# A router fed from the raw residual: logits scaled by rstd after the matmul, half of a multiply moved to GpSimd

## The reference, cut to what matters

```python
x = x + mod[:, None, 2] * y                       # y: the mixer's output
h = modulate(rmsnorm(x, norm_ffn[i]), mod[:, 3], mod[:, 4])
x = x + mod[:, None, 5] * moe(h, w_router, b_router, w_exp_gate[i], w_exp_up[i], w_exp_down[i])

def rmsnorm(x, g):  return x * rsqrt(mean(x * x, -1) + eps) * g
def modulate(h, shift, scale):  return h * (1.0 + scale) + shift

def moe(h, ...):
    scores = sigmoid(x @ w_router)                # x is h; T = 384 tokens, 16 experts
    sel = scores + b_router                       # best group of four, then its top two
    ...
    hid = silu(x @ wg[e]) * (x @ wu[e]);  y = sum_e combine[t, e] * (hid @ wd[e])
```

## Time and profile before

| | us |
|---|---|
| three runs | 1322.2, 1330.95, 1330.68; median 1330.68 |
| the profiled execution | 1324.39 |
| its span in the profile | 1322.7 |
| TensorE busy | 1200.5 (91%) |
| VectorE, ScalarE, GpSimd busy | 383.4, 316.7, 122.6 |
| mean granted TensorE clock | 0.962 of full speed |

### The profile page before, as it was taken

How to read it: one execution, slowest core, us unless ns; L and a number is a source line. 1 busy time by engine, 2 the same in 40 slices (tenths; PEclk the granted TensorE clock), 3 DMA queues, 4 the chain that set the end, 5 groups by cost and what they waited for, 6 DMA issues and landing times.

```text
span 1322.7 us, 24788 instructions
## 1 busy us (share of the span) xinstructions
PE 1200.5 (91%) x10404; PEld 697.5 (53%) x10404; DVE 383.4 (29%) x1218; ACT 316.7 (24%) x716; POOL 122.6 (9%) x188
## 2 busy tenths in 40 slices
PE   4788998789998899899978999999999997789996
PEld 2446544447885554654447643445465444565544
DVE  1345111340004522621132023341451115561113
ACT  1240111231124522211133211230411114401113
POOL 2000100210000000111020000000002111001101
PEclk9898999889999999899989999999999998989998
DMA  9999999794326873898979223891689987658993
GB/s 349 412 421 421 409 413 421 282 350 151 119 96 247 298 314 140 321 409 347 412 271 351 69 96 106 357 363 64 251 344 357 419 359 277 273 214 355 397 390 136
DMA packets 89708, 389.57 MB, mean 295 GB/s; under 512 B 10456, under 2 KB 38604, under 8 KB 53240
## 3 DMA queue, kind: packets, MB, share of 16 engines
q1 hardware_dynamic: 71568, 336.61, 65.2%
q0 software_dynamic: 17456, 51.07, 10.5%
q10 hardware_dynamic: 568, 0.23, 0.1%
HBM read 370.96 MB, written 27.96 MB: 302 GB/s over the span
## 4 chain that ended last, share of the span: by engine, by line
PE 76%; DMA 10%; DVE 5%; SPq 3%; issue 3%; ACT 2%; POOL 1%; POOLq 0%; DVEq 0%; ACTq 0%
PE bank L491 70%; DMA sb_ring<-in_w_ada 3%; PE bank L966 3%; SPq L449 2%; DMA slot_out<-sb_arena,sb_homes 2%; DMA sb_arena<-slot_out,sb_slots 2%; DMA sb_ring<-in_w_exp_up 2%; POOL sb_arena L2132 1%; DVE sb_xT L1994 1%; PE bank L984 1%; DMA slot_out<-sb_arena 1%; DMA sb_arena<-token_rows,sb_rows 1%; PE bank L894 0%; DVE sb_arena L1954 0%; PE bank L1017 0%
## 5 line engine op out<-in xcount | busy, mean ns | idle before, releaser
L491 PE MATMUL bank<-sb_ring,sb_arena 128*32 128x256 f32 (+1 forms) x6112 | 449.9, 429 | 17.3 <-DMA sb_ring<-in_w_exp_down 8.0
L491 PEld LDWEIGHTS bank<-sb_ring,sb_arena 128*32 128x32 f32 x6112 | 212.5, 111 | 197.8 <-issue 108.0
L491 PE MATMUL bank<-sb_arena 128*128 128x128 f32 (+11 forms) x776 | 140.7, 361 | 10.9 <-DVE sb_arena L1840 7.0
L491 PE MATMUL bank<-sb_ring,sb_hT 128*128 128x256 f32 x624 | 140.8, 387 | 6.2 <-ACT sb_hT L1225 6.2
L491 PEld LDWEIGHTS bank<-sb_ring,sb_hT 128*128 128x128 f32 x624 | 120.6, 194 | 26.9 <-issue 9.1
L491 PEld LDWEIGHTS bank<-sb_arena 128*128 128x128 f32 (+2 forms) x776 | 102.7, 194 | 45.6 <-issue 13.0
L491 PE MATMUL bank<-sb_ring,sb_cond 128*2 128x512 f32 x768 | 94.9, 616 | 8.8 <-DMA sb_ring<-in_w_ada 8.5
L491 PE MATMUL bank<-sb_arena,sb_ring 128*128 128x384 f32 (+2 forms) x288 | 95.5, 507 | 3.0 <-DVE sb_arena L1710 2.1
L1941 DVE TENSOR_TENSOR sb_arena<-sb_arena,bank 128x256 f32<-128x256 f32 x40 | 16.8, 421 | 248.9 <-PE bank L491 248.9
L491 PE MATMUL bank<-sb_hT,sb_ring 128*128 128x384 f32 x256 | 85.8, 498 | 2.6 <-ACT sb_hT L1225 2.6
L491 PEld LDWEIGHTS bank<-sb_arena,sb_ring 128*128 128x128 f32 (+1 forms) x288 | 49.9, 181 | 44.9 <-issue 19.0
(11 more groups left out here) (318 smaller groups left out, 1013.8 us busy)
## 6 DMA issues: line engine op xcount, KB each, us to landing
sb_ring<-in_w_ada SPq DMA_DIRECT2D x96, 1024.0 KB, 8.7
sb_ring<-in_w_exp_gate SPq DMA_DIRECT2D x60, 1024.0 KB, 10.4
sb_ring<-in_w_exp_up SPq DMA_DIRECT2D x60, 1024.0 KB, 12.7
sb_ring<-in_w_exp_down SPq DMA_DIRECT2D x60, 1024.0 KB, 15.1
sb_ring<-in_w_mlstm_in SPq DMA_DIRECT2D x12, 1024.0 KB, 12.1
token_rows<-sb_arena POOLq DMA_DIRECT2D x12, 512.0 KB, 7.6
slot_out<-sb_arena POOLq DMA_DIRECT2D x9, 512.0 KB, 8.8
sb_scratch<-in_w_exp_gate SPq DMA_DIRECT2D x4, 1024.0 KB, 9.0
```

The costliest lines, as they stand in the source:

```text
L491: return pe.matmul(out, lhsT, rhs, start=first, stop=last)
```

## The change

The router no longer waits for `hT`. A scaled router matrix `w_ra` (`w_router` times the gain, one for context and one for latents, 32 columns) is made on VectorE ahead of the residual (`router_weights`); the shift's part of the logits is made by 16 small matmuls (`shift_logits`) and kept in a row (`shift_copy`). TensorE multiplies the raw residual by `w_ra`, between the sums of squares (`raw_logits`). When `rstd` is there, VectorE multiplies the logits by it (`norm_routed`) and TensorE folds them, with the shift's part added by three matmuls. VectorE then multiplies only chunks 0 to 3 of `xT` by `rstd`, over all tokens at once, and GpSimd chunks 4 to 7 (`hp_scaled`); ScalarE applies gain and shift together (`modulate`), chunk 0 ahead of the router's exponential, the rest behind it. The turns go in the order 0, 2, 4 (chunks 0 to 3), the counts of the picks (five matmuls in place of nine), then 1, 3, 5. The modulation rows 4, 5 and 6 now stand together behind the turns. In the diff the first pieces are TensorE's, `modulate` and the `experts` below it ScalarE's, `router_weights` and the `norm_routed` below it VectorE's, and the last `experts` GpSimd's; `TURNS` is [0, 2, 4, 1, 3, 5]. Some semaphores are merged.

```diff
+            def raw_logits(L, n, a, b):
+                pe.wait_ge(wra_ready, L + 1)
+                for k in range(a, b):
+                    pe.wait_ge(x_ready, 8 * n + k + 1)
+                    q = k % 4
+                    ins = mm(ps[5][32 * q:32 * q + 32, 0:TOK], w_ra[:, k, :, :].rearrange("p c e -> p (c e)"), xT[:, k, :],
+                             k < 4, k >= 4)
+                    if k >= 4:
+                        ins.then_inc(lg_full, 1)
+
+            def shift_logits(L, bank):
+                pe.wait_ge(mod_added, 3 * L + 2)
+                for c in range(2):
+                    for k in range(KC):
+                        ins = mm(bank[0:1, c * NE:(c + 1) * NE], mod[:, L, 24 + k, c:c + 1], w_rt[:, k, :], k == 0, k == KC - 1)
+                ins.then_inc(sr_full, 1)
+
+            def norm_routed(L, n):
+                if L == 0:
+                    norm(n)
+                    ada(2, 6, 7)
+                    ada_columns(2)
+                    shift_logits(0, ps[5])
+                    raw_logits(L, n, 0, KC)
+                else:
+                    for a, b in ((0, 2), (2, 4), (4, 6), (6, 7), (7, 8)):
+                        raw_logits(L, n, a, b)
+                        norm_squares(n, a, b)
+                    norm_mean(n)
+                pe.wait_ge(sr_ready, L + 1)
+                for t in range(NT):
+                    c = min(t, 1)
+                    mm(ps[4][:, t * NE:(t + 1) * NE], ones[0:1, :], shift_row[:, c * NE:(c + 1) * NE], t == 0, False)
+                pe.wait_ge(lg_ready, L + 1 + (L > 0))
+                for t in range(NT):
+                    c = min(t, 1)
+                    ins = mm(ps[4][:, t * NE:(t + 1) * NE], lg[:, t * P:(t + 1) * P], fold[:, c * NE:(c + 1) * NE], False, t == NT - 1)
+                ins.then_inc(rt_full, 1)
...
             def pool_mixer(r):
+                if r:
+                    shift_logits(3, ps[7])
...
                 pe.wait_ge(hsT_ready, 8)
                 pe.wait_ge(n_copied, 1)
+                shift_logits(1, ps[5])
...
             def mla(r):
+                shift_logits(2, ps[7])
...
             def experts(L, n):
-                side(ps[6], w_rt, n)
-                for c in range(2 * NT):
-                    if c == 2:
-                        unfold(ps[6], L + 1 + (L > 0), rt_full)
+                def count_picks():
+                    pe.wait_ge(mask_ready, L + 1)
+                    pick = rt[:, 5, :]
+                    sums = ps[6][:, 64:64 + (NT + 1) * NE]
+                    mm(sums[:, NE:], ones[:, :], pick, True, False)
+                    mm(sums[:, 0:NE], tri[:, 0:P], pick[:, 0:NE], False, False)
+                    mm(sums[:, NE:NT * NE], tri[:, 0:P], pick[:, NE:], False, False)
+                    mm(sums[:, 2 * NE:], ones[:, :], pick[:, 0:2 * NE], False, False)
+                    mm(sums[:, NT * NE:], ones[:, :], pick[:, 0:NE], False, True).then_inc(pos_full, 1)
+
+                for c in TURNS:
+                    if c == 1:
+                        count_picks()
+                    pe.wait_ge(h_ready, 16 * n + (8 if c % 2 == 0 else 16))
+                    if c == 4:
+                        pe.wait_ge(rt_e, L + 1)
                     for k in range(4):
                         ins = pe.transpose(ps[c][:, k * P:(k + 1) * P],
                                            hT[:, 4 * (c % 2) + k, (c // 2) * P:(c // 2 + 1) * P], ident[:, :])
                     ins.then_inc(ht_full, 1)
                 for g in ADA_WINDOW[L]:
-                    ada(g, 4, 5)
...
-                for g in ADA_WINDOW[L]:
-                    ada(g, 6)
+                    ada(g, 4, 5, 6)
...
+            def modulate(L, n, a, b):
+                gain, bias = amp[:, L, 1, :, :], mod[:, L, 24:32, :]
+                for k in range(a, b):
+                    if k < KC // 2:
+                        act.wait_ge(h_scaled, 16 * n + 4 * k + 4)
+                    else:
+                        act.wait_ge(hp_scaled, KC // 2 * L + k - KC // 2 + 1)
+                    for c in range(2):
+                        o = h_out(k, c)
+                        act.activation(o, o, ACT.Identity, bias=bias[:, k, c:c + 1], scale=gain[:, k, c:c + 1]).then_inc(h_ready, 1)
...
             def experts(L, n):
+                modulate(L, n, 0, 1)
                 act.wait_ge(rt_full, L + 1)
-                act.activation(rt[:, 1, :], ps[6][:, 0:48], ACT.Exp, scale=-1.0).then_inc(rt_e, 1)
+                act.activation(rt[:, 1, :], ps[4][:, 0:48], ACT.Exp, scale=-1.0).then_inc(rt_e, 1)
+                modulate(L, n, 1, KC)
...
+            def router_weights(L):
+                for c in range(2):
+                    ins = v.tensor_tensor(w_ra[:, :, c, :], w_rt[:, :, :], amp[:, L, 1, :, c:c + 1].to_broadcast([P, KC, NE]), ALU.mult)
+                ins.then_inc(wra_ready, 1)
+
+            def norm_routed(L, n):
+                v.wait_ge(lg_full, 4 * (L + 1 + (L > 0)))
+                v.wait_ge(rstd_ready, n + 1)
+                v.tensor_tensor(lg, ps[5][:, 0:TOK], rstd[:, :], ALU.mult).then_inc(lg_ready, 1)
+                for k in range(KC // 2):
+                    v.tensor_tensor(hT[:, k, :], xT[:, k, :], rstd[:, :], ALU.mult).then_inc(h_scaled, 4)
...
             def experts(L):
+                g.wait_ge(rstd_ready, 2 * L + 2)
+                for k in range(KC // 2, KC):
+                    g.tensor_tensor(hT[:, k, :], xT[:, k, :], rstd[:, :], ALU.mult).then_inc(hp_scaled, 1)
                 for t in range(NT):
-                    g.wait_ge(ht_ready, 2 * NT * L + 2 * t + 2)
+                    g.wait_ge(ht_ready, 2 * NT * L + NT + t + 1)
                     g.dma_start(Xg[t * P:(t + 1) * P, :], htok[:, t, :]).then_inc(tokens_out, 16)
```

105 lines of the change are left out of this document (56 added, 49 removed).

## The result

The changed kernel took 1333.13 us (median of 20 runs, 1326.44 to 1341.71) beside 1322.70 for the kernel before on the same chip; the ratio is 1.0064, with a 95% interval of 1.0049 to 1.0080. The profiled execution took 1330.21 us, its span is 1328.5.

The account below looks back on a forecast made before the run. TensorE, busy 91%, was taken as the bound, with layer 0 set by DMA and layer 3's router by VectorE's chain. Layer gains 0 + 0.3 + 3.6 + 5.4 = 9.3 us off 1330.68 gave 1321, range 1308 to 1333.

Parts of the forecast that it names:

- Layer 0: 0, by the full DMA engines: Layer 0: the weight stream at 416 to 420 GB/s sets the end, so the change wins 0 us there.
- Layer 1: 0.3: Layer 1: gathering 3.2 us earlier, less 2.9 for the small matmuls of the shift, so 0.3 us won.
- Layer 2: 3.6: Layer 2: rstd 1.6 us later, yet gathering at 956.2 in place of 959.78, so 3.6 us won.
- Layer 3: 5.4: Layer 3: 5.9 from the earlier picking chain, 1.0 from counts, less 0.5 for router weights and 1.0 for clock: 5.4 us won.
- the rival of the two engines: VectorE and GpSimd multiplying beside each other wait in turn, picks come at 9.8; 2.7 us won in all, 1328; chance 0.30.
- GpSimd's product, 0.84: GpSimd's multiplies of chunks 4 to 7 by rstd: 0.84 us each, hidden while one takes under 1.5 us.
- ScalarE's instructions at 0.36: ScalarE's modulation of the chunks: 0.36 us an instruction, ending about 7.1 us behind rstd, with no turn waiting.
- Raw logits, 2.05 in layer 1, 1.6 in layer 2, hidden in layer 3: Eight extra TensorE matmuls between the squares: rstd 2.05 us later in layer 1, 1.6 in layer 2, hidden in layer 3.
- shift_logits, 2.9: Sixteen small TensorE matmuls ahead of layer 1's projection: 2.9 us on the path, bounds 2.0 and 3.5.
- TensorE keeps its clock (rival): Gathering in layers 1 and 2 keeps full clock: up to 3 us more won in each, 1315; chance 0.17.
- The weights hold the end (rival): Last expert rounds wait for weights whose stream starts no earlier: half the gain left, 1326; chance 0.08.
- The slots that come free later are harmless: Layer 1: modulation rows free their slots 4.8 us later, but the ring holds expert weights unwanted for 10 us more.

## Why the prediction was wrong

*The step that failed* is that a nearer gathering was counted as time won: of the expert stage the prediction looked at the stream of weights alone, which "starts with the ranking and moves with it", and put the path of GpSimd's stores at nothing. The prediction followed the chain to the gathering matmuls and stopped. There is a second chain: turns, ScalarE's copies, GpSimd's stores, their landing, the gather of round 1. The change shortened the first and lengthened the second, by the turns put behind the counts and by a later rstd. The diff shows it (the store waits for NT + t + 1 copies in place of 2t + 2), and I named the waiting turns only as a danger to the gathering. Of the stores' path I priced nothing, although layer 0 already waited 2.3 us at its end. The runs showed 20.6 us of waiting at that end, and with it taken out of layers 1 and 2 alone a ratio of 0.9959.

*The base.* The forecast of 1321 took 9.3 us from the median of three runs, 1330.68. The median of twenty is 1322.70; from it the same sum gives 1313.4, and the measured 1333.13 stands 19.7 above. That the number missed by 12 only is luck of the base.

*Layer 0: 0, by the full DMA engines.* Lost 3.3 us, 3.0 of them by the start of round 1. The full stream did not protect it.

*Layer 1: 0.3.* Won 2.2 to the next norm (0.7 and 1.7 in the other two executions), with 4.0 us of waiting in it.

*Layer 2: 3.6.* Lost 7.0; its gathering came 2.9 us nearer to the norm.

*Layer 3: 5.4.* Won 1.6. The gathering is 15.9 us behind rstd (18.4 before), 2.5 won, less 0.6 by which rstd comes later. The chain begins at 5.56, not 3.0: the rival of the two engines, chance 0.30, was right in mechanism and size (picks done at 9.8 forecast, 10.1 measured). Its total of 1328 fell to the same missing chain.

*GpSimd's product, 0.84.* 0.99 alone, 1.30 beside VectorE. VectorE's product, alone, 0.49, as forecast.

*ScalarE's instructions at 0.36.* 0.45 apart; with gain and shift both as columns one of 128 columns takes 485 ns, with the shift alone 388. Its chunks end at 9.8, not 7.1, and "no turn waits for them" did not hold: turns 0, 2 and 4 waited 1.4 us for chunks in layer 1 and 4.2 in layer 3. Turns 1, 3 and 5 found theirs ready by 0.2 us, as the picks too came late. The Trainium skill's ScalarE: Activation LUTs (What ACT_TABLE_LOAD costs) has this price, about 93 ns for each such operand; the trace gives 97, and I had left it out.

*Raw logits, 2.05 in layer 1, 1.6 in layer 2, hidden in layer 3.* The stretch of the squares grew from 1.86 to 2.8 us in layer 1, and rstd came 1.1 us later (5.65 behind the first of them, before 4.59); in layers 2 and 3 it came 0.6 later (4.80 behind the last residual, before 4.17), so it was not hidden in layer 3. *shift_logits, 2.9.* 0.95. *router_weights, 0.5.* 0.48:

```profile
1119.54 0.95 PE L495 MATMUL bank<-sb_w_rt,sb_mod 128*1 128x16 f32 x32
...
1139.45 0.48 DVE L1611 TENSOR_TENSOR sb_w_ra<-sb_w_rt,sb_amp 128x128 f32<-128x128 f32 x2
```

*TensorE keeps its clock (rival).* True of the gathering in layers 0 to 2, 6.86 us in place of 8.8 to 9.4; but the modulation rows behind the fold ran at half clock in layer 2, and the time saved was spent in the wait for rows.

*The weights hold the end (rival).* TensorE waited for expert weights 2.0, 2.2 and 2.4 us in layers 1 to 3, before 2.1, 1.9 and 2.5, so no new wait came there; in layer 0 it was 13.8 for 8.4, but 10.4 and 9.8 in the two other executions.

*The slots that come free later are harmless.* Not so: nobody missed those weights, but their loads ran beside the stores, and with them held the last stores of layers 1 and 2 landed in 7.5 and 5.4 us.

## What to carry to other kernels

When a step gets earlier, follow every chain that meets it again, through memory too: a store, its landing and the gather behind it were 26 us here in layer 0, and the chain that the change was about, from rstd to the gathering, took 15.5 to 18.5. A DMA that someone waits for competed in layers 1 and 2 with the loads issued around it, so look at what frees their buffers, and when. And fill the engine's idle time with work that was on the path; do not put new work between the steps of that path.

## What the runs showed of the hardware

In layer 3, with no loads beside them, the three stores of 512 KB landed in 3.0, 4.7 and 6.1 us in the changed kernel (2.9, 3.5 and 3.8 before). In layer 0 the last of three took 15.1 to 15.9 in every kernel with the late stores, on GpSimd's queue or ScalarE's, with 3 to 5 loads of 1 MB issued in the 16 us ahead of the first. The Trainium skill's DMA: Bandwidth & Descriptors (Queues, rings and completion order) says that a DMA engine takes the queues it has work for in turn, packet by packet. If that gave two queues even shares of the 420 GB/s measured there, 1.5 MB would take 7.5 us, an estimate, which layer 0 does not bear out.

Within the 20 runs of the changed kernel the time fell by 8.9 us for 0.01 of mean granted clock (0.945 to 0.960), in 30 runs of the kernel before by 8.2 (0.954 to 0.966). The changed kernel's mean is 0.005 lower on both chips where both were recorded, which by these slopes is an estimate of 4 us beside a loss of 3.5 and 8.0. Which is cause and which effect the runs do not say: in its profile the clock fell to 0.50 in each of the three waits for rows, of 4.0 to 8.6 us, while in layer 1 waits of 1.2, 1.4 and 2.2 us passed at full clock, and in layer 2 the clock fell behind a wait of 1.1.
